# Moving the pooling of a two-block network onto TensorE and reordering its mixer stage

## The chip, the cores and the metric

The kernel runs on one core of a Trainium2 chip. TensorE (PE) does matrix products, VectorE (DVE) and GpSimd (POOL) work on elements, ScalarE (ACT) evaluates functions and copies, SyncE (SP) starts the DMAs that bring weights. The metric is the device time of one execution in microseconds (us). Every engine has its own in-order queue; the queues meet through semaphores only.

## The reference, cut to what matters

Two blocks of two layers each work on one sequence of 512 positions with 1024 channels, in float32. The first block (attention of three kinds) isn't touched except by the padding. In the second block each layer is a feed-forward part, the mixer and a second feed-forward part, each followed by a layer norm. The mixer is what the change concerns:

```python
h = x @ w_in[l]                       # 1024 -> 512 (u) + 4 x 512 (q, f, v, g)
u = h[..., :D_POOL]
q, f_raw, v, g = jnp.split(h[..., D_POOL:], 4, axis=-1)
y_pool = multiscale_pool(u, pool_w[l], pool_scale[l])
o = hgrn2_recurrence(q, f_raw, v, lb_all[l])
y_hgrn = head_rms_norm(o, hgrn_norm_g[l]) * jax.nn.silu(g)
mix = jnp.concatenate([y_pool, y_hgrn], axis=-1) @ w_out[l]
# multiscale_pool, group i of 128 channels, window w = 2, 4, 8, 16:
#   (mean of the last min(w, t+1) positions of u) - u, then a 128x128 product, then a scale per channel
# hgrn2_recurrence, per head: S_t = diag(f_t) S_(t-1) + (1 - f_t) outer v_t;  o_t = S_t^T q_t
```

## The kernel before, in words

Activations lie channels on partitions, positions along the free axis. Each large product is made of tiles of 128 output channels by 512 positions. Weights and activations are split into a high and a low float32r part, and a tile takes three matmuls per 128 input channels (three_products, lines 214, 215 and 217), so 24 for the mixer's input (DC = 8). SP fetches weight tiles into a ring of four, DVE splits them two tiles ahead (split_tile, lines 167 and 169), PE multiplies, and in the mixer ACT copies tile i out of bank 6 or 7 into p2 (line 1583). A tile may start when its weights are split and the tile two before it has been copied.

The mixer has 20 input tiles (N_IN2), in the order f (0 to 3), q (4 to 7), v (8 to 11), u (12 to 15, the pooled half), g (16 to 19). Between the tiles every engine does parts of the recurrence, at tile numbers written out by hand ("if i == 13"). The recurrence is computed in four chunks of 128 positions per head. Inside a chunk, decays are handled at seven levels of block sizes LEVELS = (64, 32, 16, 8, 4, 2, 1): DVE subtracts (sub, line 1690), ACT takes exponentials (level_exps, lines 1578 and 1579), DVE multiplies (level, lines 1708 and 1709), and PE forms scores: two top levels of large pieces (top_level, line 1840) and six masked levels (masked_level, line 1860, 64 small matmuls each, five of the levels and the diagonal of k and q), which DVE adds up under masks (accumulate, lines 1716 to 1720) and then copies into place (line 1806). The keys are turned by PE (line 1899) and multiplied with the values (line 1906), DVE chains the states of the chunks (lines 1791 and 1797). Then PE makes the outputs o of four heads (lines 1918 and 1920), ACT squares them (line 1665), PE sums the squares (line 1924), ACT takes logarithm and exponential for the root (lines 1668 and 1672), DVE multiplies (line 1823), ACT and DVE split into high and low (lines 1676 and 1810), and PE multiplies the first two tiles of w_out (lines 214 to 217 again): chunks k = 0 to 3 are the pooled half, 4 to 7 the four heads.

In this kernel the masked levels start only after the last input tile. The pooling is POOL's: from line 1948 it makes the decayed keys, then per group shifted additions, scale and edge correction and the subtraction (lines 1959 to 1968), each waiting for the one before; PE multiplies each group (pool_product, line 1867), and ACT scales it into p2 (line 1637). PE's order after the last tile is: four pool products, masked levels 0 and 1, keys turned, levels 2 and 3, key-value products, levels 4 and 5, outputs and sums, the first two tiles of w_out.

The helper sb in hybrid_kernel pads each named buffer to a multiple of LINE floats, here 32 (128 bytes). In the compiled kernel before, x, xh and xl (and ones) start at 128 bytes past a multiple of 256, and the weight parts two_hi and two_lo, the feed-forward activations hh and hl and the mixer's buffers start at a multiple of 256: the small buffer eps with its padding takes 128 bytes.

Of the kernel before, what the change touches and what calls it, by code (L numbers as in the profile page):

```python
# [21 lines left out]
ALU = mybir.AluOpType  # L22
# [52 lines left out]
M_INV = M_MASK + 32 * len(MASKED)  # L75
N_K2 = M_INV + HH * PADT

# [4 lines left out]
LINE = 32  # L82
# [1425 lines left out]

def mixers(kit, ctx, l, before):

# [4 lines left out]
    def sb(name, shape):  # L1515
# [5 lines left out]
    vrow = sb("vrow", [P, NT, HH, P])  # L1521


    v_place = p2[:, D_V:D_V + HH, :].rearrange("p h t -> p (h t)")
    at = v_place.rearrange("p (n h t) -> p n h t", n=NT, h=HH)
    pl = v_place[:, 0:2 * (PADT + T)].rearrange("p (s t) -> p s t", s=2)

    kd = p2[:, D_F:D_F + HH, :].rearrange("p h t -> p (h t)")

    kr = kd.rearrange("p (n h c) -> p n h c", n=NT, h=HH)  # L1530
    qe = bb[:]

    ad, tm = (kit.ln[:, i, :].rearrange("p (a t) -> p a t", t=32) for i in range(2))
    sta = sb("sta", [P, 3, HH, P])
    el = sb("el", [P, NT * HH])
    lbv = sb("lbv", [P, 6, HH])
# [3 lines left out]
    k_banks = (bank[6], bank[7], bank[3])  # L1540
    s = kit.sems("mix", DENSE + APPLY_SEMS + ("chain_v", "abs_f", "exp_f", "ln_f", "ls_made", "km_made", "k_made", "a_made", "m_made", "lb_in",
                         "lb_act", "lb_made", "e2", "e3", "e4", "b_made", "sub_made", "exp_made", "top_mm", "last_sub", "ke_exp", "sc_kept", "lv_made",
                         "lev_mm", "acc_made", "at_made", "v_turned", "v_kept", "qe_exp", "qe_made", "kd_made",
                         "k_turned", "k_kept", "kv_mm", "st_made", "o_mm", "o_kept", "osq_made", "o_summed",
                         "oln_made", "orstd_made", "y_made", "g_made", "u_pad", "pool_chain", "pooled", "p_mm",
                         "hi_made", "p_kept", "lo_made", "ylo_made", "zeroed"))
# [6 lines left out]
    rst = df[:, 0, :]  # L1553

# [10 lines left out]
    def scalar(a):  # L1565
# [6 lines left out]
        a.activation(lbv[:, 1, :], lbv[:, 1, :], ACT.Exp, scale=-1.0).then_inc(s["lb_act"], 1)  # L1572

        def level_exps(i):
# [4 lines left out]
            a.activation(left, left, ACT.Exp, scale=-1.0).then_inc(s["exp_made"], 1)  # L1579

        for i in range(N_IN2):
# [8 lines left out]
            if i == 4:  # L1590
                a.wait_ge(s["lb_act"], 2)
                a.activation(lbv[:, 1, :], lbv[:, 1, :], ACT.Ln, bias=kit.ones[:, 0:1]).then_inc(s["lb_act"], 1)
                a.wait_ge(s["exp_f"], 1)
                a.activation(df[:, 0, :], df[:, 0, :], ACT.Ln, bias=kit.ones[:, 0:1]).then_inc(s["ln_f"], 1)
            if i == 5:
# [6 lines left out]
            if i == 6:  # L1602
                a.wait_ge(s["e2"], HH)
                a.activation(df[:, 1, :], df[:, 1, :], ACT.Exp, scale=-1.0).then_inc(s["e3"], 1)
            if i == 7:
# [5 lines left out]
            if i == 8:  # L1611
                a.wait_ge(s["e3"], 1)
                a.activation(df[:, 1, :], df[:, 1, :], ACT.Ln, bias=kit.ones[:, 0:1]).then_inc(s["e4"], 1)
            if i == 12:
                level_exps(0)

                for n in range(NT):
                    a.wait_ge(s["v_turned"], n + 1)
                    a.activation(vrow[:, n, :, :], bank[n][:].rearrange("p (h c) -> p h c", h=HH), ACT.Copy
                                 ).then_inc(s["v_kept"], 1)  # L1620
            if i == 13:
                level_exps(1)
            if i == 14:

                a.wait_ge(s["last_sub"], 1)
                a.activation(v_place, v_place, ACT.Exp).then_inc(s["ke_exp"], 1)
                a.activation(el[:], bb[:, P - 1:W:P], ACT.Exp).then_inc(s["ke_exp"], 1)
            if i == 15:
# [623 lines left out]
```

## Time and profile before

| | before |
|---|---|
| median of 3 runs | 2828.55 us (2828.39 to 2829.93) |
| the profiled execution | 2831.76 us |
| its span, first to last instruction | 2830.0 us |
| mean granted TensorE clock | 0.958 of full speed |
| PE busy | 2630.8 us (93%) |
| DVE, ACT, POOL busy | 48%, 26%, 24% |

Times in the rows are us from the first instruction. A row of a timeline holds consecutive instructions of one line: the start, the time from the first start to the last end, the engine, the line, the operation, what it writes and reads, the shapes and their number; in brackets the idle time of the engine before it and what ended that. A float32 matmul (not float32r) counts as two instructions. In a row of a stretch each engine has its busy time and its instructions in brackets, and PEclk is the granted TensorE clock as a share of 2.4 GHz.

### The profile page before, as it was taken

How to read it: one execution, taken by the hardware profiler on the slowest of the kernel's cores; microseconds unless marked ns; L12 is line 12 of the kernel's file. 1: busy time of each engine (PE TensorE's matmuls, PEld its weight loads, DVE VectorE, ACT ScalarE, POOL GpSimd, SP SyncE). 2: the span in 40 equal slices, each digit the busy share in tenths (PEclk: the TensorE clock that was granted, in tenths of full speed). 3: DMA queues.
4: the chain of work that ended last, by engine and by line, in shares of the span. 5: the costliest groups of instructions: out<-in, count | busy, mean ns of one | idle time of the engine just before them, and what ended most of it. 6: DMA issues, size and time to landing. Idle time of an engine off the chain costs nothing. (4 is left out here: it accounts for less than half of the span.)

```text
span 2830.0 us, 36447 instructions
## 1 busy us (share of the span) xinstructions
PE 2630.8 (93%) x13232; PEld 2086.7 (74%) x13232; DVE 1367.0 (48%) x2271; ACT 727.9 (26%) x1465; POOL 685.3 (24%) x422
## 2 busy tenths in 40 slices
PE   7989888989879999997799999899999987999997
PEld 4867756867648888876678888788888765788886
DVE  4356834367653334467653333533344575633344
ACT  2135621156431110042431110211110424311101
POOL 1000031000223331117243331233311163433311
PEclk9998989979989999999899999999999997999999
DMA  5310013300122333221122333133332220223332
GB/s 193 97 45 1 2 60 126 96 1 2 38 89 92 94 102 102 78 84 58 39 81 90 96 108 102 56 97 96 99 103 88 75 67 31 79 93 96 103 103 80
DMA packets 57268, 222.22 MB, mean 79 GB/s; under 512 B 6664, under 2 KB 7816, under 8 KB 56768
## 3 DMA queue, kind: packets, MB, share of 16 engines
q1 hardware_dynamic: 56000, 214.01, 23.7%
q10 hardware_dynamic: 1152, 6.68, 0.6%
q8 instruction: 72, 1.18, 0.2%
q14 instruction: 44, 0.36, 0.0%
HBM read 218.51 MB, written 2.15 MB: 78 GB/s over the span
## 5 line engine op out<-in xcount | busy, mean ns | idle before, releaser
L214 PE MATMUL bank<-xh,two_hi 128*128 128x512 f32 x1856 | 741.5, 400 | 37.7 <-ACT xh L1173 33.7
L215 PE MATMUL bank<-xh,two_lo 128*128 128x512 f32 x1856 | 737.8, 398 | 0.0
L217 PE MATMUL bank<-xl,two_hi 128*128 128x512 f32 x1856 | 727.0, 395 | 0.0
L167 DVE CAST two_hi<-two_raw 128x1024 fp32r<-128x1024 f32 (+1 forms) x292 | 228.3, 782 | 952.7 <-PE bank L217 950.7
L214 PEld LDWEIGHTS bank<-xh,two_hi 128*128 128x128 f32 x1856 | 352.5, 190 | 129.3 <-issue 36.6
L215 PEld LDWEIGHTS bank<-xh,two_lo 128*128 128x128 f32 x1856 | 352.8, 190 | 82.0 <-issue 0.5
L217 PEld LDWEIGHTS bank<-xl,two_hi 128*128 128x128 f32 x1856 | 351.0, 189 | 82.7
L169 DVE TENSOR_TENSOR two_lo<-two_raw,two_hi 128x1024 fp32r<-128x1024 f32 (+1 forms) x292 | 395.5, 1355 | 10.0
L1395 POOL TENSOR_TENSOR up_hm<-up_sg,up_hm 128x512 f32<-128x512 f32 x88 | 197.9, 2249 | 581.2 <-ACT up_hm L1377 581.2
L214 PE MATMUL bank<-hh,two_hi 128*128 128x512 f32 x704 | 276.3, 392 | 0.0
L217 PE MATMUL bank<-hl,two_hi 128*128 128x512 f32 x704 | 274.1, 389 | 0.0
L215 PE MATMUL bank<-hh,two_lo 128*128 128x512 f32 x704 | 274.0, 389 | 0.0
L214 PE MATMUL bank<-xh,onein_hi 128*128 128x512 f32 x384 | 154.3, 402 | 16.6 <-ACT xh L470 15.8
L1377 ACT ACTIVATE up_hm<-bank 128x512 f32<-128x512 f32 x88 | 52.8, 600 | 428.1 <-PE bank L217 428.1
L215 PE MATMUL bank<-xh,onein_lo 128*128 128x512 f32 x384 | 153.7, 400 | 0.0
L215 PEld LDWEIGHTS bank<-hh,two_lo 128*128 128x128 f32 x704 | 132.1, 188 | 28.4 <-issue 1.0
L214 PEld LDWEIGHTS bank<-hh,two_hi 128*128 128x128 f32 x704 | 132.2, 188 | 28.1 <-issue 1.0
L217 PEld LDWEIGHTS bank<-hl,two_hi 128*128 128x128 f32 x704 | 132.1, 188 | 27.7
L217 PE MATMUL bank<-xl,onein_hi 128*128 128x512 f32 x384 | 150.7, 398 | 1.5 <-POOL xl L500 1.5
L1398 POOL TENSOR_TENSOR hl<-up_hm,hh 128x512 f32 x88 | 115.0, 1307 | 83.7 <-ACT hh L1379 83.7
L937 ACT ACTIVATE w<-w,negm 128x128 f32<-128x128 f32 (+4 forms) x192 | 94.9, 494 | 97.2 <-DVE negm L880 96.1
L1379 ACT ACTIVATE hh<-up_hm 128x512 f32 x88 | 55.7, 633 | 216.1 <-POOL up_hm L1395 216.1
(314 smaller groups left out, 3185.6 us busy)
## 6 DMA issues: line engine op xcount, KB each, us to landing
two_raw<-in_up SPq DMA_DIRECT2D x180, 512.0 KB, 3.6
two_raw<-in_down SPq DMA_DIRECT2D x64, 704.0 KB, 4.0
one_raw<-in_w_in SPq DMA_DIRECT2D x52, 512.0 KB, 3.6
two_raw<-in_w_in SPq DMA_DIRECT2D x40, 512.0 KB, 3.6
one_raw<-in_w_out SPq DMA_DIRECT2D x16, 512.0 KB, 3.6
two_raw<-in_w_out SPq DMA_DIRECT2D x16, 512.0 KB, 3.7
w<-in_w ACTq DMA_DIRECT2D x2, 2048.0 KB, 10.6
x<-in_x SPq DMA_DIRECT2D x1, 2048.0 KB, 8.3
```

The lines of the kernel that those rows point to most:

```text
L167: v.tensor_copy(st.hi[:, h, 0:w], st.raw[:, r, 0:w]).then_inc(st.hi_made, 1)
L169: v.tensor_tensor(st.lo[:, h, 0:w], st.raw[:, r, 0:w], st.hi[:, h, 0:w].bitcast(F32), ALU.subtract).then_inc(st.w_split, 1)
L214: pe.matmul(out[:], wh, xh[:, kx, :], start=start, stop=False)
L215: pe.matmul(out[:], wl, xh[:, kx, :], start=False, stop=False)
L217: return pe.matmul(out[:], wh, xl[:, kx, :], start=False, stop=stop)
L937: a.activation(row, row, ACT.Exp, bias=negm[:, i:i + 1], scale=-1.0, accum_out=tot[:, i:i + 1]).then_inc(s["exps"], 1)
L1377: a.activation(hm[:, f, :], bank[1][:], ACT.Copy).then_inc(s["out_taken"], 1)
L1379: a.activation(hh[:, bass.ds(j * 2 + f, 1), :].rearrange("p o t -> p (o t)"), hm[:, f, :], ACT.Copy).then_inc(s["hhi_made"], 1)
L1395: g.tensor_tensor(hm[:, f, :], sg[:, f, :], hm[:, f, :], ALU.mult).then_inc(s["h_made"], 1)
L1398: g.tensor_tensor(hl[:, at, :].rearrange("p o t -> p (o t)"), hm[:, f, :], hh[:, at, :].rearrange("p o t -> p (o t)").bitcast(F32), ALU.su ...
```

## The change

The pooling becomes products on TensorE. A constant kb (128 x 4 x 272 floats, fetched by ACT's DMA queue at tile 8) holds for each window the banded matrix "mean minus token": one for the first chunk, one for the others, and 16 columns for what spills from the chunk before. pool_weights multiplies u by the group's weights first (16 matmuls of 128x128), ACT copies the four banks into p2, and pool_steps then applies the band: per group four matmuls of 128 columns and three of 16. The scaled result is taken straight from PSUM by ACT (high part) and DVE (low part). POOL loses the pooling, the decayed keys (now 16 exponentials on ACT with a bias and one product on DVE), the product of q with its decay (now DVE) and the low parts; it keeps two memsets.

The masked levels move between the input tiles, one after each of tiles 14 to 18, in the order of levels 2, 3, the diagonal, 4, 5, 6; one remains after tile 19. Values are turned after tiles 12 and 13, keys after tile 16, pool_weights after tile 17. DVE's and ACT's steps move up accordingly. The last accumulate writes into place directly. After the state chain PE makes chunks k = 0 to 3 of the first two w_out tiles, then the heads' outputs and sums (two banks instead of four for the sums, so a sum waits for the logarithm two before it), then k = 4 to 7. ACT takes logarithm, exponential and high part head by head instead of in three rounds. PE's loop over tiles 8 to 11 is written out. LINE becomes 64 (256 bytes).

Of the diff, the lines that matter (removed lines are left out where the step only moved):

```diff
-LINE = 32
+LINE = 64
...
+    MASKED_LEVELS = (2, 3, None, 4, 5, 6)
+    MASK_OF = (0, 1, 5, 2, 3, 4)
...
             if i == 8:
+                a.dma_start(kb[:], kit.d["kb"]).then_inc(s["steps"], 16)
+                a.wait_ge(s["b_made"], HH * NT)
+                for b in range(HH * NT):
+                    c = slice(b * P, (b + 1) * P)
+                    a.activation(kd[:, c], bb[:, c], ACT.Exp, scale=-1.0, bias=bb[:, b * P + P - 1:b * P + P]
+                                 ).then_inc(s["ke_exp"], 1)
+                a.activation(el[:], bb[:, P - 1:W:P], ACT.Exp).then_inc(s["ke_exp"], 1)
+                level_exps(0)
+            if i == 9:
+                level_exps(1)
+            if i == 11:
+                level_exps(2)
             if i == 12:
+                level_exps(3)
+                keep_values(0)
+                keep_values(1)
+            if i == 13:
+                keep_values(2)
+                keep_values(3)
+                level_exps(4)
+            if i == 14:
+                level_exps(5)
+            if i == 15:
+                a.wait_ge(s["zeroed"], 2)
+                a.wait_ge(s["top_mm"], 2 * NT)
                 for n in range(NT):
+                    top = bank[n][:].rearrange("p (h t) -> p h t", h=HH)
+                    a.activation(at[0:64, n, :, 64:128], top[0:64, :, 64:128], ACT.Copy).then_inc(s["at_made"], 1)
+                    a.activation(at[0:32, n, :, 32:64], top[0:32, :, 32:64], ACT.Copy).then_inc(s["at_made"], 1)
+                    a.activation(at[64:96, n, :, 96:128], top[64:96, :, 96:128], ACT.Copy).then_inc(s["at_made"], 1)
+            if i == 16:
+                a.wait_ge(s["k_turned"], NT - 1)
+                for n in range(NT - 1):
+                    a.activation(kr[:, n, :, :], bank[n][:].rearrange("p (h c) -> p h c", h=HH), ACT.Copy
+                                 ).then_inc(s["k_kept"], 1)
             if i == 17:
+                level_exps(6)
+                a.activation(qe, bb[:], ACT.Exp).then_inc(s["qe_exp"], 1)
+                a.wait_ge(s["z_mm"], NT)
+                for n in range(NT):
+                    a.activation(zt[:, n, :], bank[n][:], ACT.Copy).then_inc(s["z_kept"], 1)
...
+        for c in range(HH):
+            a.wait_ge(s["p_mm"], c + 1)
+            a.activation(kit.xh[:, c, :], bank[6 + c % 2][:], ACT.Copy, scale=kit.s2[:, Q_PS + c:Q_PS + c + 1]
+                         ).then_inc(s["hi_made"], 1)
...
+            if i == 8:
                 v.wait_ge(s["b_made"], HH * NT)
                 v.wait_ge(s["k_made"], HH)
                 sub(0)
+            if i == 9:
                 sub(1)
                 v.wait_ge(s["out_taken"], 2 + D_Q + HH)
                 level(0)
+            if i == 10:
+                level(1)
+            if i == 11:
+                sub(2)
+                sub(3)
+            if i == 12:
+                level(2)
+                v.wait_ge(s["ke_exp"], HH * NT)
+                v.tensor_tensor(kd, kk[:], kd, ALU.mult).then_inc(s["kd_made"], 1)
+            if i == 13:
+                level(3)
+                sub(4)
             if i == 14:
+                sub(5)
             if i == 15:
+                level(4)
+                accumulate(0)
             if i == 16:
+                level(5)
+                accumulate(1)
             if i == 17:
+                sub(6)
+                accumulate(2)
             if i == 18:
+                level(6)
+                accumulate(3)
             if i == 19:
+                v.wait_ge(s["qe_exp"], 1)
+                v.tensor_tensor(qe, qe, q, ALU.mult).then_inc(s["qe_made"], 1)
+                accumulate(4)
+        accumulate(5)
...
+        for c in range(HH):
+            v.wait_ge(s["hi_made"], c + 1)
+            v.scalar_tensor_tensor(kit.xl[:, c, :], bank[6 + c % 2][:], kit.s2[:, Q_PS + c:Q_PS + c + 1],
+                                   kit.xh[:, c, :].bitcast(F32), ALU.mult, ALU.subtract).then_inc(s["lo_made"], 1)
...
+        def turn_keys():
+            pe.wait_ge(s["kd_made"], 1)
+            pe.wait_ge(s["at_made"], 3 * NT)
+            for n in range(NT - 1):
+                for h in range(HH):
+                    mm = pe.transpose(bank[n][:, h * P:(h + 1) * P], kd[:, cols(h, n)], ident)
+                mm.then_inc(s["k_turned"], 1)
+        def pool_weights():
+            pe.wait_ge(s["k_kept"], NT - 1)
+            pe.wait_ge(s["out_taken"], 2 + D_U + HH)
+            for n in range(NT):
+                for c in range(HH):
+                    mm = pe.matmul(bank[n][:, c * P:(c + 1) * P], p2[:, D_U + c, n * P:(n + 1) * P],
+                                   kit.s2[:, Q_PW + c * P:Q_PW + (c + 1) * P], start=True, stop=True)
+                mm.then_inc(s["z_mm"], 1)
+        def pool_steps(c):
+            out = bank[6 + c % 2]
+            for n in range(NT):
+                first = FIRST_STEP if n == 0 else INNER_STEP
+                mm = pe.matmul(out[:, n * P:(n + 1) * P], zt[:, n, c * P:(c + 1) * P], kb[:, c, first:first + P],
+                               start=True, stop=n == 0)
+                if n:
+                    mm = pe.matmul(out[:, n * P:n * P + PADT], zt[:, n - 1, c * P:(c + 1) * P],
+                                   kb[:, c, SPILL_STEP:SPILL_STEP + PADT], start=False, stop=True)
+            mm.then_inc(s["p_mm"], 1)
...
+        dense_products(pe, st, s["out_taken"], l, "w_in_2", DC, kit.xh, kit.xl, dense_banks, first=D_Q, last=D_V)
+        for i in range(D_V, N_IN2):
             dense(i)
+            if i == 11:
+                top_level(0)
+            if i == 12:
+                top_level(1)
+                turn_values(0)
+                turn_values(1)
+            if i == 13:
+                turn_values(2)
+                turn_values(3)
+            if i == 14:
+                masked_level(0)
+            if i == 15:
+                masked_level(1)
+            if i == 16:
+                masked_level(2)
+                turn_keys()
+            if i == 17:
+                masked_level(3)
+                pool_weights()
+            if i == 18:
+                masked_level(4)
+        masked_level(5)
+        pe.wait_ge(s["z_kept"], NT)
         for n in range(NT - 1):
             for h in range(HH):
+                mm = pe.matmul(bank[n][:, h * P:(h + 1) * P], kr[:, n, h, :], vrow[:, n, h, :], start=True, stop=True)
             mm.then_inc(s["kv_mm"], 1)
+        pe.wait_ge(s["steps"], 16)
+        pe.wait_ge(s["out_taken"], 2 + N_IN2)
+        for c in range(HH):
+            if c >= 2:
+                pe.wait_ge(s["lo_made"], c - 1)
+            pool_steps(c)
+        after = base + N_IN2
+        def out_products(k):
+            for u in range(2):
+                mm = three_products(pe, st, bank[u], u, k, kit.xh, kit.xl, k, k == 0, k == DC - 1)
+                if k == DC - 1:
+                    mm.then_inc(st.mm_done, 1)
+        def sum_squares(h):
+            pe.wait_ge(s["osq_made"], h + 1)
+            if h >= 2:
+                pe.wait_ge(s["oln_made"], h - 1)
+            pe.matmul(bank[6 + h % 2][:], kit.ones[:], osq[:, h * T:(h + 1) * T], start=True, stop=True
+                      ).then_inc(s["o_summed"], 1)
+        pe.wait_ge(st.w_split, st.split_after(l, after + 1))
         pe.wait_ge(s["st_made"], 1 + 2 * HH)
+        for k in range(HH):
+            pe.wait_ge(s["lo_made"], k + 1)
+            out_products(k)
         pe.wait_ge(s["qe_made"], 1)
         pe.wait_ge(s["at_made"], 3 * NT + 4)
         for h in range(HH):
             for n in range(NT):
+                out = bank[2 + h][:, n * P:(n + 1) * P]
                 mm = pe.matmul(out, vrow[:, n, h, :], at[:, n, h, :], start=True, stop=n == 0)
                 if n:
                     mm = pe.matmul(out, sta[:, n - 1, h, :], qe[:, cols(h, n)], start=False, stop=True)
             mm.then_inc(s["o_mm"], 1)
             if h:
+                sum_squares(h - 1)
+        sum_squares(HH - 1)
+        for k in range(HH, DC):
+            pe.wait_ge(s["ylo_made"], k - HH + 1)
+            out_products(k)
...
-        for i, w in enumerate(POOL_WINDOWS):
-            u = p2[:, D_U + i, :]
-            g.wait_ge(s["out_taken"], 2 + D_U + i + 1)
-            link(g.tensor_tensor(pl[:, 0, PADT + 1:], u[:, 1:], u[:, :T - 1], ALU.add))
-            for j in range(1, i + 1):
-                a_, b_ = pl[:, (j - 1) % 2, :], pl[:, j % 2, :]
-                link(g.tensor_tensor(b_[:, PADT:], a_[:, PADT:], a_[:, PADT - 2 ** j:PADT + T - 2 ** j], ALU.add))
-            m = pl[:, i % 2, PADT:]
-            link(g.tensor_scalar(m[:, PADT:], m[:, PADT:], 1.0 / w, None, ALU.mult))
...
-            g.tensor_tensor(u, m, u, ALU.subtract).then_inc(s["pooled"], 1)
-            g.wait_ge(s["pooled"], i + 1)
...
+        inside = (a <= b) & (a > b - w)
+        kb[:, i, FIRST_STEP:FIRST_STEP + P] = inside * (f32(1) / np.minimum(b + 1, w).astype(f32)) - (a == b)
+        kb[:, i, INNER_STEP:INNER_STEP + P] = inside * (f32(1) / f32(w)) - (a == b)
+        kb[:, i, SPILL_STEP:] = (a > P + np.arange(PADT)[None, :] - w) * (f32(1) / f32(w))
```

## Rows read from the trace of the kernel before

**Rows 1.** The page: busy time of each engine, share of span, instructions.
```profile
PE 2630.8 (93%) x13232; PEld 2086.7 (74%) x13232; DVE 1367.0 (48%) x2271; ACT 727.9 (26%) x1465; POOL 685.3 (24%) x422
```

**Rows 2.** Stretches, PE alone: both layers' time from tile 19 to w_out.
```profile
1325.20:1399.20 74.00, 46.22 (x924) 0.77 0.01 2
2322.00:2397.00 75.00, 46.78 (x925) 0.75 0.01 2
```

**Rows 3.** Timeline of ACT: input tiles 18 and 19 copied out, layer 0.
```profile
1319.66 0.60 ACT L1583 ACTIVATE p<-bank 128x512 f32<-128x512 f32 x1 [4.42 <-PE bank L217]
1325.23 0.60 ACT L1583 ACTIVATE p<-bank 128x512 f32<-128x512 f32 x1 [4.98 <-PE bank L217]
```

**Rows 4.** A stretch of all engines (PE, PEld, DVE, ACT, POOL, PEclk) after tile 19.
```profile
1330.00:1345.00 15.00, 3.19 (x4) 1.00 (x4) 4.26 (x2) 0.69 (x1) 14.06 (x14) 0.57 0.00 0
```

**Rows 5.** Timeline of POOL: the last step of the pooling.
```profile
1342.57 1.26 POOL L1968 TENSOR_TENSOR p<-p 128x512 f32<-128x512 f32 x1
```

**Rows 6.** Timeline of PE after the pooling: masked levels, then the first output.
```profile
1346.74 3.14 PE L1860 MATMUL bank<-xx 128*32 128x32 f32 x234 [0.78 <-ACT p L1637]
...
1361.29 0.75 PE L1860 MATMUL bank<-xx 128*32 128x32 f32 x35 [2.59 <-issue]
...
1366.93 1.26 PE L1860 MATMUL bank<-xx 128*32 128x32 f32 x126
...
1370.84 0.72 PE L1860 MATMUL bank<-p,kk 128*32 128x32 f32 x60 [2.02 <-issue]
1375.56 1.20 PE L1918 MATMUL bank<-p,vrow 128*128 128x128 f32 x4 [4.00 <-DVE p L1806]
```

**Rows 7.** Timeline of ACT and PE: outputs, root, and the last matmul of w_out.
```profile
1383.52 0.60 ACT L1665 ACTIVATE xx<-bank 128x512 f32<-128x512 f32 x1 [1.82 <-PE bank L1920]
1385.94 0.60 ACT L1665 ACTIVATE xx<-bank 128x512 f32<-128x512 f32 x1 [1.82 <-PE bank L1920]
1386.43 2.42 ACT L1668 ACTIVATE df<-bank,eps 128x512 f32<-128x512 f32 x4
...
1383.32 1.02 PE L1924 MATMUL bank<-xx,ones 128*128 128x512 f32 x2
...
1398.46 0.39 PE L217 MATMUL bank<-xl,two_hi 128*128 128x512 f32 x1
```

**Rows 8.** Timeline of DVE: a split, a sub, masked add, copy into place, states.
```profile
1280.89 0.69 DVE L167 CAST two_hi<-two_raw 128x1024 fp32r<-128x1024 f32 x1
...
1282.76 2.28 DVE L1690 TENSOR_TENSOR df<-bb 128x2048 f32<-128x2048 f32 x1
...
1368.49 2.35 DVE L1797 SCALAR_TENSOR_TENSOR sta<-sta,el,bank 128x128 f32<-128x128 f32 x8
1370.76 0.68 DVE L1718 TENSOR_TENSOR ln<-bank,k 128x512 f32<-128x512 f32 x1
...
1373.65 1.77 DVE L1806 COPY p<-ln 32x512 f32<-32x512 f32 x4
```

**Rows 9.** Timeline of ACT: one function of a 128x2048 buffer between tiles 8 and 9.
```profile
1258.98 2.00 ACT L1613 ACTIVATE df<-df,ones 128x2048 f32<-128x2048 f32 x1
```

**Rows 10.** Stretches of all engines around a layer norm: PE's pause and what follows.
```profile
1200.50:1205.50 5.00, 1.86 (x9) 1.33 (x9) 3.77 (x9) 4.12 (x11) 2.35 (x1) 1.00 0.14 34
1205.50:1209.00 3.50, 3.40 (x9) 2.20 (x10) 3.43 (x6) 3.45 (x7) 2.56 (x3) 0.56 0.27 107
```

**Rows 11.** DMA queues from 1340 to 1380 us: packets and MB that bring instructions.
```profile
q8 instruction: 6, 0.10, 1.0%
```

**Rows 12.** Timeline of PE, a feed-forward down product; the second is 24 matmuls later.
```profile
1120.29 0.39 PE L214 MATMUL bank<-hh,two_hi 128*128 128x512 f32 x1
...
1125.73 0.39 PE L214 MATMUL bank<-hh,two_hi 128*128 128x512 f32 x1
```

**Rows 13.** The page's costliest groups: dense matmuls by what they read, count, mean ns.
```profile
L214 PE MATMUL bank<-xh,two_hi 128*128 128x512 f32 x1856 | 741.5, 400 | 37.7 <-ACT xh L1173 33.7
...
L214 PE MATMUL bank<-hh,two_hi 128*128 128x512 f32 x704 | 276.3, 392 | 0.0
```

More of the change, by code:

```diff
@@ L1539, in mixers @@
     dense_banks = bank[6:8]
[L1540 to L1546, printed above, removed]
+    s = kit.sems("mix", DENSE + APPLY_SEMS + (
+        "chain_v", "abs_f", "exp_f", "ln_f", "ls_made", "km_made", "k_made", "a_made", "m_made", "lb_in", "lb_act", "lb_made",
+        "e2", "e3", "e4", "b_made", "sub_made", "exp_made", "top_mm", "ke_exp", "lv_made", "lev_mm", "acc_made", "at_made",
+        "v_turned", "v_kept", "qe_exp", "qe_made", "kd_made", "k_turned", "k_kept", "kv_mm", "st_made", "o_mm", "o_kept",
+        "osq_made", "o_summed", "oln_made", "orstd_made", "y_made", "g_made", "z_mm", "z_kept", "p_mm", "hi_made",
+        "lo_made", "ylo_made", "zeroed", "steps"))
     q = p2[:, D_Q:D_Q + HH, :].rearrange("p h t -> p (h t)")
@@ L1752, in vector @@
                 v.tensor_tensor(df[:, 0, :], df[:, 0, :], df[:, 1, :], ALU.add).then_inc(s["a_made"], 1)
-            if i == 10:
+            if i in (6, 7):
                 v.wait_ge(s["a_made"], 1)
-                for h in range(HH):
+                for h in ((0, 1) if i == 6 else (2, 3)):
                     for n in range(NT):
@@ L1870, in tensor @@
         dense_on_arrival(pe, st, s, l, "w_in_2", DC, kit.xh, kit.xl, dense_banks,
                          lambda k: wait_high(pe, s, k), lambda k: wait_low(pe, s, k))
-        dense_products(pe, st, s["out_taken"], l, "w_in_2", DC, kit.xh, kit.xl, dense_banks, first=D_Q, last=D_U)
-        dense(D_U)
-        pe.wait_ge(s["out_taken"], 2 + D_V + HH)
-        for n in range(NT):
-            for h in range(HH):
-                mm = pe.transpose(bank[n][:, h * P:(h + 1) * P], p2[:, D_V + h, n * P:(n + 1) * P], ident)
-            mm.then_inc(s["v_turned"], 1)
@@ L1897, in tensor @@
+        masked_level(5)
+        pe.wait_ge(s["z_kept"], NT)
         for n in range(NT - 1):
             for h in range(HH):
-                mm = pe.transpose(k_banks[n][:, h * P:(h + 1) * P], kd[:, cols(h, n)], ident)
-            mm.then_inc(s["k_turned"], 1)
-        masked_level(2)
-        masked_level(3)
-        for n in range(NT - 1):
-            pe.wait_ge(s["k_kept"], n + 1)
-            for h in range(HH):
-                mm = pe.matmul(bank[n][:, h * P:(h + 1) * P], kr[:, n, h, :], vrow[:, n, h, :],
-                               start=True, stop=True)
-            mm.then_inc(s["kv_mm"], 1)
@@ L1916, in tensor @@
             for n in range(NT):
-                out = bank[h][:, n * P:(n + 1) * P]
+                out = bank[2 + h][:, n * P:(n + 1) * P]
                 mm = pe.matmul(out, vrow[:, n, h, :], at[:, n, h, :], start=True, stop=n == 0)
@@ L1922, in tensor @@
             if h:
-                pe.wait_ge(s["osq_made"], h)
-                pe.matmul(bank[4 + h - 1][:], kit.ones[:], osq[:, (h - 1) * T:h * T], start=True, stop=True
-                          ).then_inc(s["o_summed"], 1)
-        pe.wait_ge(s["osq_made"], HH)
-        pe.matmul(bank[4 + HH - 1][:], kit.ones[:], osq[:, (HH - 1) * T:HH * T], start=True, stop=True
-                  ).then_inc(s["o_summed"], 1)
-        after = base + N_IN2
-        pe.wait_ge(st.w_split, st.split_after(l, after + 1))
```

234 lines of the change are left out of this document (72 added, 162 removed).

## The prediction, made before the changed kernel ran

> **What bounds the kernel now.** I read the page first: PE is busy for 2630.8 of 2830.0 us, 93% [rows 1], so only time in which PE waits, or work taken off it, can be won. The change puts work onto PE. It can pay only where PE stands still now, and the second view, stretches of PE, shows where: from the end of input tile 19 to the first two tiles of w_out the mixer takes 74 us per layer, of which PE is busy 46, at a mean clock of 0.77, and both layers look the same [rows 2]. Third, ACT's timeline dates the tiles: a tile is copied as soon as PE ends it, 18 at 1319.66 and 19 at 1325.23, so one tile is 5.57 us, 24 matmuls of 0.232 us, with no wait between them [rows 3]. Before the tail PE is full; the tail is where it waits.
>
> Fourth, what the tail waits for. From 1330 to 1345 POOL is busy 14.06 of 15 us and PE 3.19, at clock 0.57 [rows 4]: the pooling is the bound. Its last step ends at 1343.8 [rows 5], and only then do the masked levels start, at 1346.7 [rows 6]. From there it is a chain over PE, DVE and ACT with PE mostly at the lower clock: the first output product starts at 1375.56, after 4.00 us of waiting for DVE's last copy [rows 6], and w_out's last matmul ends near 1398.7 [rows 7]. So the tail is 1325.2 to 1398.7, 73.5 us: 50.3 up to the first output, 23.1 from there.
>
> **The change part by part, per layer.** I take the tail apart and build the new one from its rows.
>
> 1. The pooling leaves the path. This removes POOL's wait, PE's four full-width pool products, and the idle time in which the clock fell.
>
> 2. Five masked levels move between tiles 14 to 18. They go where PE is full, so they cost their whole time. A level is 128 instructions. At the full clock 126 of them take 1.26 us, and 234 at a mostly lower one 3.14, or 1.7 per 128 [rows 6]. With some 0.3 for the change of shape I take 1.6 us each: 8.0 us (bounds 6.5 and 10.5). Turning the keys is 12 and pool_weights 32 instructions of 128 columns. The price of one comes from the outputs: heads follow each other every 2.42 us [rows 7], which is 14 such instructions and a sum of squares of about 0.87, so 0.11 us each: 1.3 and 3.5 us. Together 12.9 us.
>
> 3. Instruction supply. The masked levels stop twice for "issue", 2.59 and 2.02 us [rows 6], and 0.10 MB of instructions arrives in six packets in 40 us [rows 11]; a level is 256 instructions with its weight loads. Between dense tiles there is time to fetch, yet one level and a tile are 152 pairs in 7.2 us. Bounds: nothing, or 2.6 us for each of three stops, 7.8. I take 2.0, nearer to nothing, since the dense parts give the fetch about 5.6 us each. So tile 19 ends 14.9 us later than now, near 1340.1.
>
> 4. Do DVE and ACT keep up in the loop? A split takes 1.87 us from start to start [rows 8], a sub or any product over 2048 columns 2.28 [rows 8], an ACT function of that size 2.0 [rows 9]. I let each queue run from tile 3: the tightest place is the split of tile 8, due at 1252.9 and done near 1252.5 after a chain of ACT (exponential, logarithm, absolute value, exponential, logarithm) and DVE's sum; later the worst step on DVE is a split with two subs, 6.4 us, against a tile period that by then has grown to 7 us or more. So I cost this at nothing, with a bound of 3 us if each handoff is slower. ACT's fetch of kb is one DMA issue beside a queue that DMA does not bound, and has 80 us to land: nothing. The two memsets left on POOL are done long before ACT asks for them.
>
> 5. From tile 19 to the outputs. PE needs a masked level (1.6), 24 key-value instructions (2.7) and two pool_steps (8 instructions of 128 columns and 6 of 16, I take 1.2 each). DVE is later: split 1.9, the product of q 2.3, accumulate(4) 1.4, accumulate(5) 0.7 + 1.8, states 0.7 + 2.4, first low part 0.7, in all 11.9 us [rows 8]. pool_steps(2) waits for that low part (lo_made), so PE idles some 5 us here; then pool_steps(2) and (3) 2.4, and 24 matmuls of w_out's pooled half 5.6. At a layer norm PE is busy 1.86 of 5 us, and in the 3.5 us after that the clock is 0.56, near the lower of its two levels (1.2 and 2.4 GHz) [rows 10], so I add 2.0 for a slow start. Sum: 11.9 + 2.4 + 5.6 + 2.0 = 21.9 us; the outputs start near 1362.
>
> 6. From the outputs to the end. Four heads with sums: the last square starts 8.0 us in (now 10.4, because the first two heads run at the lower clock). Then ACT works head by head: logarithm, exponential, high part, 0.6 us each [rows 7] with small handoffs, 1.85 per head; the low part of the last head is ready at about 16.7. The sum of head 2 waits for the logarithm of head 0 behind all four squares, about 1.3 us, which this chain hides. The last chunk of w_out is 1.4 us more, handoffs 0.2. PE idles in pieces, so 1.0 for some time at the lower clock: 19.3 us (bounds 18.3 and 21.5). Now it is 23.1. The pooled half of w_out no longer covers the root, but it would not have been needed: PE now runs its 48 products without a gap, and after the change only the last is behind the root's chain.
>
> Sum per layer: 14.9 + 21.9 + 19.3 = 56.1 against 73.5, a gain of 17.4 us; two layers 34.8. The profiled execution took 2831.76 us, 1.8 more than its span and 3.2 more than the median; the gain does not depend on that, so from the median: 2828.5 - 34.8 = **2793.7**.
>
> 7. The padding. It moves every buffer behind eps by 128 bytes against multiples of 256: the weight parts and hh and hl, not xh and xl. The trace shows two speeds of the same dense matmul. Reading hh, 24 take 5.44 us, 0.2267 each [rows 12]; reading xh, 0.232 [rows 3], and the page's mean durations agree, 392 against 400 ns [rows 13]. Before, hh starts at a multiple of 256 and xh 128 bytes past one. If the moving operand's start decides, hh becomes slow too: 3 x 704 = 2112 matmuls by 5.5 ns, 12 us lost. If it is that both operands share the same remainder, xh becomes fast: at least 3 x 1856 = 5568 by 5.5 ns, 31 us gained, and more with the first block. If it is something else (the loops differ, and so does where the buffers lie), nothing. I take nothing, because no row separates these, and keep both ends.
>
> A rule that speaks against step 2: the Trainium skill, "TensorE: Matmul & The Clock Gate", section "Wait — 56ns, not 53.3ns?", states that matmuls never start closer than about 25 ns however small they are. By it a level would be at least 3.2 us, the five moved ones 16 instead of 8, and the forecast 16 us higher for both layers, an estimate of 2810. The trace's 126 instructions in 1.26 us, 10 ns apart, speak against the rule here [rows 6].
>
> **The rivals.** A, the other speed: the padding slows hh's products. For it: the only buffers at a multiple of 256 that are read as moving operand by dense matmuls are the fast ones. Against: the code around them differs as well. It gives 2793.7 + 12 = 2806. B, the padding speeds up xh's: 2793.7 - 31 = 2763 or a little less. C, the small matmuls don't fit between the tiles: fetch stops of 7.8 us instead of 2.0, levels at 2.1 us (2.5 more), 3 us of DVE and ACT being late: 11.3 per layer more, 2816. For it: the stops in rows 6; against: dense tiles of 5.6 us beside each level. D, slower than before: the coupled queues. ACT now holds waits for DVE (sub_made, b_made) in front of the copy that frees PE's bank, and DVE holds waits for ACT and PE in front of the split PE needs. If a handoff is late in each turn, PE loses it at every tile: the gain of 17.4 per layer is eaten once each of the 15 tiles from 5 to 19 is late by more than 1.2 us; at 1.6 us the kernel is at 2828.5 + 2 x (15 x 1.6 - 17.4) = 2842. Against: before, with the same ring, the tiles show no such wait [rows 3], and by hand each queue arrives before it is due. E, it doesn't do what it says, the pooling stays the bound: excluded, as POOL's pooling is gone.
>
> **How the numbers follow.** Forecast with a neutral padding 0.54, A 0.18, B 0.12, C 0.10, D 0.06. The forecast's own bounds, steps 2, 3, 5 and 6, are about 5 us per layer to either side, 2783 to 2804. The range takes in A and C and the lower side of the forecast and leaves out B and D: 2776 to 2816. A difference of 0.2% is 5.7 us, about what a measurement of this kernel can tell from none. Faster by over 0.2% means under 2822.9: all of the forecast, A, B and most of C, 0.91; within 0.2% 0.04; slower 0.05.
>
> **What would show it.** Tile 19 should be copied about 15 us later after tile 11 than now, with tile periods near 7.2 us at tiles 15 to 18; a period over 9 us means C or D, and the wait before line 217 or 214 then names DVE or ACT. PE should idle some 5 us before pool_steps(2), waiting for DVE, and the time from tile 19's copy to w_out's last matmul should be near 41 us. Of the padding, the start-to-start time of dense matmuls reading hh (0.2267) and xh (0.232) decides A and B at once. The prediction would be wrong above all if those change, or if PE is stopped for instructions beside the dense tiles.

## The result and the profile after

The changed kernel takes 2759.84 us, the median of five runs (2757.37 to 2764.68). The kernel before, in five runs beside it, takes 2829.2 (2828.39 to 2831.14). The ratio is 0.976, with a 95% interval of 0.9746 to 0.9773: 69.4 us gained, twice the forecast 34.8, and 16 us below the lower end of the range. The profiled execution took 2759.84, its span is 2758.1 us and the mean granted clock 0.964.

The page of the kernel after. The engine line answers to [rows 1], the groups to [rows 13].

```profile
PE 2595.6 (94%) x13392; PEld 2090.5 (76%) x13392; DVE 1355.0 (49%) x2281; ACT 735.0 (27%) x1495; POOL 560.4 (20%) x354
...
L213 PE MATMUL bank<-xh,two_hi 128*128 128x512 f32 x1856 | 734.8, 396 | 40.6 <-ACT xh L1172 33.9
L214 PE MATMUL bank<-xh,two_lo 128*128 128x512 f32 x1856 | 729.2, 393 | 0.0
...
L213 PE MATMUL bank<-hh,two_hi 128*128 128x512 f32 x704 | 276.2, 392 | 0.0
```

PE has 160 instructions more and is yet busy 35 us less. Moving work onto PE can't do that, and the mean clock is hardly higher (0.964 for 0.958). The same work has become cheaper: the mean of the xh group fell from 400 to 396 ns, the hh group stayed at 392. The mean duration hides the size, since a matmul overlaps the next. The start-to-start time shows it, here from the timeline of PE of the kernel after, two rows 24 matmuls apart:

```profile
1489.26 0.39 PE L216 MATMUL bank<-xl,two_hi 128*128 128x512 f32 x1
...
1494.70 0.39 PE L216 MATMUL bank<-xl,two_hi 128*128 128x512 f32 x1
```

That is 5.44 us, 0.2267 each, where a tile on xh took 5.57 before [rows 3]. The speed that hh alone had [rows 12] is now everybody's. A weight load takes 190 ns in the mean in both kernels; only the spacing has changed.

The stretches of all engines from tile 19's copy to the mixer's end, for both layers (columns PE, PEld, DVE, ACT, POOL, then PEclk), answer to [rows 2]:

```profile
1317.70:1364.00 46.30, 37.60 (x321) 31.06 (x320) 22.87 (x35) 17.23 (x24) 0.00 (x0) 0.85 0.00 1
2283.70:2329.90 46.20, 37.68 (x320) 31.09 (x318) 22.86 (x35) 17.23 (x24) 0.00 (x0) 0.85 0.00 1
```

The tail is 46.3 and 46.2 us instead of some 74, the clock 0.85 instead of 0.77 and 0.75, and POOL does nothing in it. I cut layer 0's mixer into four pieces, from tile 3's copy to the first addition of the next phase: tiles 3 to 11, 44.8 us before and 44.0 after; tiles 11 to 19, 49.9 and 61.0; tile 19 to the outputs, 50.3 and 26.8; the outputs to the next phase, 23.6 and 19.6. Together 168.7 and 151.4, a gain of 17.4. This includes the faster matmuls: 384 for tiles 4 to 19 and 48 for w_out, by 5.5 ns, would be 2.4 us, which leaves 15.0 for the reordering. Measured at equal padding, from tile 3's copy to ACT's first table load of the next phase, it gains a little more. With the new padding (the padding alone against the changed kernel, both run below) the two layers take 166.5 and 167.2 us, and 151.3 both: 15.2 and 15.9. With the old one (the kernel before against the reordering alone) they take 168.7 and 168.6, and 152.2 and 152.9: 16.4 and 15.7. So the reordering is worth 31 to 32 us in all. The other 37 to 38 us of the 69.4 fall to the padding, and the count agrees within 2 us: 7104 matmuls on xh and xl (3 x 1856, 3 x 384 and 384 of w_out in the first block) by 5.5 ns are 39.1.

### The profile page after: what moved, and what is told of

It is laid out like the page before. It is cut to its first block and busy times, and to the rows that moved or that the text cites. A ratio compares the mean times of both kernels' runs of the same rounds, so it can differ in the third digit from the quotient of the medians.

```text
span 2758.1 us, 36735 instructions
## 1 busy us (share of the span) xinstructions
PE 2595.6 (94%) x13392; PEld 2090.5 (76%) x13392; DVE 1355.0 (49%) x2281; ACT 735.0 (27%) x1495; POOL 560.4 (20%) x354
## 5 line engine op out<-in xcount | busy, mean ns | idle before, releaser
L214 PE MATMUL bank<-xh,two_lo 128*128 128x512 f32 x1856 | 729.2, 393 | 0.0
L216 PE MATMUL bank<-xl,two_hi 128*128 128x512 f32 x1856 | 718.4, 391 | 0.0
L166 DVE CAST two_hi<-two_raw 128x1024 fp32r<-128x1024 f32 (+1 forms) x292 | 218.9, 750 | 916.8 <-PE bank L216 915.1
L213 PE MATMUL bank<-xh,onein_hi 128*128 128x512 f32 x384 | 152.3, 397 | 17.3 <-ACT xh L469 16.4
L214 PEld LDWEIGHTS bank<-hh,two_lo 128*128 128x128 f32 x704 | 132.2, 188 | 28.3 <-issue 1.0
L214 PE MATMUL bank<-xh,onein_lo 128*128 128x512 f32 x384 | 151.4, 394 | 0.0
```

Source lines behind the costliest of these rows:

```text
L166: v.tensor_copy(st.hi[:, h, 0:w], st.raw[:, r, 0:w]).then_inc(st.hi_made, 1)
L213: pe.matmul(out[:], wh, xh[:, kx, :], start=start, stop=False)
L214: pe.matmul(out[:], wl, xh[:, kx, :], start=False, stop=False)
L216: return pe.matmul(out[:], wh, xl[:, kx, :], start=False, stop=stop)
```

## The experiments

**The theories.** Theory 1: a dense matmul is fast when its moving operand and its weights start at the same remainder of 256 bytes. Theory 2: it is the moving operand's start alone that counts (rival A of the prediction). Theory 3: the speed belongs to the loops, and the padding does nothing. Before, xh and xl start 128 bytes past a multiple of 256, and the weights and hh at one. In the changed kernel all of them start 128 past.

**The padding alone**, in the kernel before:

```diff
-LINE = 32
+LINE = 64
```

> The kernel before with the 256-byte padding alone: xh and the weight parts now both start 128 bytes past a multiple of 256. Theory (equal remainders of both operands make the dense matmul fast): all 7104 dense matmuls that read xh or xl go from about 0.232 to 0.2267 us, hh's stay at 0.2267, and the kernel gains 7104 x 0.0057 = 40 us, to about 2790. Rival A (a moving operand that starts at a multiple of 256 is fast): hh goes to 0.232, xh stays, 12 us slower, 2841. Rival neutral: the gain lies in the mixer alone, 2829.

Measured: 2792.5 us against 2826.54 of the kernel before on the same chip, ratio 0.9882 (0.9853 to 0.991). PE of this kernel, two rows 24 matmuls apart, 5.44 us:

```profile
1489.23 0.39 PE L217 MATMUL bank<-xl,two_hi 128*128 128x512 f32 x1
...
1494.67 0.39 PE L217 MATMUL bank<-xl,two_hi 128*128 128x512 f32 x1
```

One constant gives half of the gain: 34.0 us, with an interval of 25 to 42 that holds the 39.1 of the count. Theory 3 falls.

**The reordering alone**, in the changed kernel:

```diff
-LINE = 64
+LINE = 32
```

> The changed kernel with the old 128-byte padding. Theory (the padding is worth about 40 us and the mixer what was forecast): dense matmuls on xh back at 0.232, total near 2829 - 33 = 2796, mixer stage 15 to 17 us shorter per layer than before. Rival (all of the gain is the mixer): 2760. The sum of this gain and that of the padding alone should be the whole 69 us if the two don't depend on each other.

Measured: 2797.5 us, ratio 0.99 (0.9869 to 0.993), that is 28.3 us gained (20 to 37). 24 matmuls on xh are back at 5.58 us:

```profile
1489.13 0.40 PE L214 MATMUL bank<-xh,two_lo 128*128 128x512 f32 x1
...
1494.71 0.39 PE L214 MATMUL bank<-xh,two_lo 128*128 128x512 f32 x1
```

The two halves multiply to 0.978, beside 0.976 measured for both together: they hardly touch each other. The forecast's 34.8 for the reordering is inside the interval, but the 31 to 32 of the traces are nearer to its middle.

**Everything at a multiple of 256** (the kernel before, with 256-byte padding):

```diff
+        ctx.enter_context(nc.sbuf_tensor("lead", [P, 32], F32))
         kit.x = sb(ctx, "x", [P, DC, T])
```

> The kernel before with 256-byte padding and 128 bytes ahead of x, so that x, xh, xl, the weight parts and hh all start at a multiple of 256. Theory of equal remainders: as with the padding alone, 2790, every dense matmul at 0.2267. Rival (it is the remainder 128 of the weight parts, or of all, that makes it fast): xh's matmuls slow at 0.232 or hh's changed, and 2829 or more.

Measured: 2791.05 us, ratio 0.9885 (0.9855 to 0.9915), the same as with everything 128 past. The absolute remainder is worth nothing.

**xh at a multiple of 256, weights and hh 128 past** (the kernel before with the lead buffer alone):

```diff
 LINE = 32
...
+        ctx.enter_context(nc.sbuf_tensor("lead", [P, 32], F32))
         kit.x = sb(ctx, "x", [P, DC, T])
```

> The kernel before with 128 bytes ahead of x alone, which moves everything by 128: x, xh, xl start at a multiple of 256, the weight parts and hh 128 bytes past one. The distance between xh and the weights is as before, both absolute starts are exchanged. Theory of equal remainders: as before, 2829, xh at 0.232, hh at 0.2267. Rival A (moving operand at a multiple of 256 is fast): xh at 0.2267, hh at 0.232, gain 40 - 12 = 28 us, 2801.

Measured: 2827.7 us, ratio 0.9995 (0.9975 to 1.0014). xh, now at the remainder that theory 2 calls the good one, stays slow, 5.58 us for 24, and hh, now at the bad one, stays fast, since it moved together with its weights. Theory 2 falls.

```profile
1489.28 0.40 PE L217 MATMUL bank<-xl,two_hi 128*128 128x512 f32 x1
...
1494.86 0.39 PE L217 MATMUL bank<-xl,two_hi 128*128 128x512 f32 x1
```

**hh moved away from its weights**, in the kernel with 256-byte padding:

```diff
+        ctx.enter_context(sb(f"hpad{i}", [P, 32], F32))
         self.hh = ctx.enter_context(sb(f"hh{i}", [P, FC, T], F32R))
```

> The padding alone, with 128 bytes more ahead of hh: hh and hl start at a multiple of 256, the weight parts 128 bytes past one, xh as with the padding alone. Theory (it is the distance between the moving operand and the weights, modulo 256, whichever buffer moves): the 2112 dense matmuls that read hh go from 0.2267 to about 0.232, those on xh stay at 0.2267, and the kernel is 2112 x 0.0057 = 12 us slower than with the padding alone, near 2804. Rival (what was slow belongs to xh or to the weights alone): hh stays fast, 2792.

Measured: 2798.08 us, ratio 0.99 (0.9886 to 0.9915). The trace is sharper than the medians. This is PE in a down product, where 24 matmuls took 5.44 us before [rows 12] and now take 5.58:

```profile
1110.07 0.39 PE L217 MATMUL bank<-hl,two_hi 128*128 128x512 f32 x1
...
1115.65 0.40 PE L217 MATMUL bank<-hl,two_hi 128*128 128x512 f32 x1
```

For 2112 matmuls that is 12 us. The medians stand 5.6 us above those of the padding alone, and the two intervals overlap, so the cost in total time is less well known than its sign in the trace.

**Distances other than 128**, in the kernel with 256-byte padding: weights 64 bytes from xh, and 32 from hh.

```diff
+        ctx.enter_context(sb(f"hpad{i}", [P, 8], F32))
...
-        kit.eps = sb(ctx, "eps", [P, 2])
+        kit.eps = ctx.enter_context(nc.sbuf_tensor("eps", [P, 2], F32))
+        ctx.enter_context(nc.sbuf_tensor("eps_pad", [P, 8], F32))
```

> The padding alone, but the buffers behind eps start 64 bytes past xh's remainder modulo 256 (192 against 128), and hh 32 bytes past the weights'. Theory 1 (any distance that is no multiple of 256 costs): both kinds of matmul at 0.232 or slower, the kernel near 2792 + 52 = 2844. Theory 2 (only a distance of 128 modulo 256 costs): both at 0.2267, 2792. Theory 3 (smaller distances cost more, the old padding to 128 was a cure for that): both above 0.235, 2860 or more.

Measured: 2850.01 us, ratio 1.0077 (1.0062 to 1.0092), slower than the kernel before. PE on xl, and in a down product on hh, each two rows 24 matmuls apart, 5.60 us both:

```profile
1489.29 0.39 PE L217 MATMUL bank<-xl,two_hi 128*128 128x512 f32 x1
...
1494.89 0.39 PE L217 MATMUL bank<-xl,two_hi 128*128 128x512 f32 x1
...
1110.26 0.40 PE L214 MATMUL bank<-hh,two_hi 128*128 128x512 f32 x1
...
1115.86 0.40 PE L214 MATMUL bank<-hh,two_hi 128*128 128x512 f32 x1
```

All 9216 dense matmuls at 6.7 ns more than 0.2267 would be 61 us over the kernel with the padding alone; measured are 57.5. So 32 and 64 bytes cost at least as much as 128. Of the distances run (0, 32, 64 and 128 bytes, modulo 256) only 0 is fast.

**The first pause in the tail.** PE stood 5.94 us before pool_steps(2). Theory: groups 2 and 3 reuse banks 6 and 7, so they wait for lo_made, and the low part stands on DVE behind the product of q, two accumulates and the states. Rival: the pause costs nothing, since the outputs wait for DVE's accumulates anyhow. Two edits take it away in different ways. First, four banks instead of two:

```diff
+    pool_bank = (bank[6], bank[7], bank[3], bank[4])
...
-            out = bank[6 + c % 2]
+            out = pool_bank[c]
...
-            if c >= 2:
-                pe.wait_ge(s["lo_made"], c - 1)
+            if c == 3:
+                pe.wait_ge(s["acc_made"], 8)
```

> The changed kernel, but the four pooled groups go to four PSUM banks (6, 7, 3, 4) instead of 6 and 7 in turn, so pool_steps(2) and (3) no longer wait for a low part. Theory (PE's pause of 5.9 us before pool_steps(2) and the lower clock after it cost about 10 us per layer): the two steps run at full clock before the pause, but PE then still waits for DVE's states and first low part, so the outputs start about 6 us earlier per layer, 2760 - 12 = 2748. Rival (DVE's chain is the bound, the pause only moves): 0 to 4 us in all.

Measured: 2747.69 us, ratio 0.9717 (0.9699 to 0.9736). The four pool_steps run through, and the wait is now behind them; PE's first matmul of w_out, and PE by stretches (busy, then PEclk):

```profile
1332.06 0.47 PE L213 MATMUL bank<-xh,two_hi 128*128 128x512 f32 x1 [2.31 <-DVE xl L1842]
...
1330.00:1335.00 5.00, 2.94 (x9) 0.79 0.02 3
1335.00:1340.00 5.00, 5.00 (x25) 0.87 0.00 0
```

The pause fell from 5.94 to 2.31 us, and the clock in the 5 us that hold it and in the next 5 is 0.79 and 0.87 instead of 0.50 for 10 us. The rival falls.

**DVE's order**, with the banks as they were: the states and the low parts before accumulate(5) and the product of q, which the outputs alone need.

```diff
             if i == 19:
-                v.wait_ge(s["qe_exp"], 1)
-                v.tensor_tensor(qe, qe, q, ALU.mult).then_inc(s["qe_made"], 1)
                 accumulate(4)
-        accumulate(5)
...
+        accumulate(5)
+        v.wait_ge(s["qe_exp"], 1)
+        v.tensor_tensor(qe, qe, q, ALU.mult).then_inc(s["qe_made"], 1)
```

> The changed kernel with another order on DVE after tile 19: accumulate(4), states, low parts of the pooled half, and only then accumulate(5) and the product of q. Theory (DVE's place for the low part is what PE waits for): the pause before pool_steps(2) all but goes, the clock stays up, the outputs start near 1335 instead of 1344.5, bound by the product of q; 10 us per layer, 2740. Rival (the outputs are bound by DVE's sum of work in any order): under 3 us per layer, 2755.

Measured: 2750.06 us, ratio 0.9723 (0.9702 to 0.9743). Here PE's clock stays at 1.00 and the pause before pool_steps(2) is gone, but the median is no better than with four banks, and half of what was expected beyond the changed kernel is missing. From ACT's table load after tile 19 to that of the next phase are 37.7 us instead of 45.7, so the trace has 16 us for both layers where the ratios have some 10. The table below shows that the tail is not where the rest went. The product of q is now the last before the outputs, as the bracket says:

```profile
1339.71 0.71 PE L2005 MATMUL bank<-p,vrow 128*128 128x128 f32 x4 [1.76 <-DVE bb L1842]
```

**Both edits together.**

> Both edits, four banks and the other order on DVE. Theory: hardly more than the order alone, 2738, since the first low part comes before pool_steps(2) would wait. If the banks alone had shown most of the gain, this should be about as fast as that.

Measured: 2743.04 us (2740.95 to 2743.41), ratio 0.97 (0.9684 to 0.9716), the best kernel of this study. Its stretch from tile 19 to the mixer's end:

```profile
1313.80:1350.90 37.10, 32.49 (x320) 26.34 (x313) 22.85 (x35) 17.18 (x24) 0.00 (x0) 1.00 0.00 1
```

It is 37.1 us instead of 46.3, and with the same work PE's busy time fell from 37.60 to 32.49. Of the 9.2 us, 5.1 are that the same instructions ran at the full clock, and the other 4.1 are idle time gone.

The medians of these kernels mix the tail with differences of some us that arise elsewhere. The traces keep them apart. The tail, from tile 19's copy to ACT's first table load of the next phase, in us:

| kernel | layer 0 | layer 1 | tile 19 copied, layer 0 | median |
|---|---|---|---|---|
| changed | 46.3 | 46.3 | 1317.75 | 2759.84 |
| four banks | 39.8 | 39.8 | 1318.92 | 2747.69 |
| DVE's order | 38.3 | 38.3 | 1321.08 | 2750.06 |
| both edits | 37.2 | 37.2 | 1313.75 | 2743.04 |
| pooled half behind (next) | 45.3 | 45.4 | 1310.18 | 2760.46 |

No edit acts before tile 19 of layer 0, and yet its copy lies at times up to 11 us apart in these executions. In the tail, DVE's order is 1.5 us per layer better than four banks, and both together gain only 1.1 more per layer, as was expected ("hardly more than the order alone"). The 7 us between the medians of the last two edits are mostly not the tail's.

**The pooled half behind the heads.** The change's description says "ahead"; is the order itself worth anything? In the changed kernel the 24 matmuls of chunks 0 to 3 go behind the last sum of squares.

```diff
-        for k in range(HH):
-            pe.wait_ge(s["lo_made"], k + 1)
-            out_products(k)
-
+        pe.wait_ge(s["lo_made"], HH)
...
         sum_squares(HH - 1)
+        for k in range(HH):
+            pe.wait_ge(s["lo_made"], k + 1)
+            out_products(k)
```

> The changed kernel with the products of w_out's pooled half behind the outputs and sums, as before the change. Theory by the rows: the outputs start 6 us earlier but at the lower clock, and the 24 products then fill part of the root's chain and end 4 to 5 us after it: 2760 within 4 us, so putting them ahead is worth nothing by itself. Rival 1 (ahead is worth its place, since it warms the clock and leaves only the last chunk behind the root): 4 to 6 us slower per layer, 2770. Rival 2 (they are better hidden behind the outputs): 3 to 5 us faster per layer, 2752.

Measured: 2760.46 us, ratio 0.9768 (0.9751 to 0.9785): no difference from the changed kernel. In the traces the tail is 0.9 us per layer shorter, which is too little for the medians to show. Behind, the pooled half covers the root's chain; ahead, it covers DVE's last steps. That the two holes are about equal is read from the times, no run took one of them away. PE starts its outputs with a row that the changed kernel doesn't have there; the second row is DVE's last low part:

```profile
1331.09 1.19 PE L2002 MATMUL bank<-p,vrow 128*128 128x128 f32 x4 [1.72 <-issue]
...
1330.13 0.75 DVE L1841 SCALAR_TENSOR_TENSOR xl<-bank,s,xh 128x512 fp32r<-128x512 f32 x1 [2.24 <-ACT xh L1682]
```

The bracket says "issue", but the edit makes PE wait for that low part (lo_made, HH) before the outputs. The low part ends at 1330.88, and PE starts 0.21 us later. So this pause is a wait for DVE and not one of the stops that step 3 priced.

## Why the prediction was wrong

**The step that failed is 7, the padding.** It laid out three cases, gave the price of each, took "nothing, because no row separates these", and chose a range that left B out. B is what happened. Its price was also short: it counted the 5568 matmuls of the second block at 31 us and put the first block's 1536 down as "and more"; they add 8.4. With 31 to 32 for the reordering and 39.1 by count for the padding, the median before of 2828.5 gives 2757 to 2758, where 2759.84 was measured.

Could the rows have decided it? Two facts were at hand: the same dense matmul, engine, line and shape has two speeds [rows 12 and 3], and the difference that could be read off the operands was the remainder, unequal for the slow ones and equal for the fast. A neutral padding left 5.5 ns on each of several thousand matmuls without a mechanism. A chance of 0.12 for B against 0.54 for "neutral" treated the lack of a separating row as evidence for zero. It was evidence for none of the three.

**The reordering, step by step.** The mechanism was right: the pooling left the path, and each later piece sits where it was put. Sizes, per layer, read in layer 0:

Step 1, right. POOL is at 20% and is idle in the tail.

Step 2, nearly right: 12.2 measured, 12.9 forecast. In the timeline of PE of the kernel after, in the loop:

```profile
1285.18 1.30 PE L1907 MATMUL bank<-xx 128*32 128x32 f32 x128
1292.08 1.30 PE L1907 MATMUL bank<-p,kk 128*32 128x32 f32 x128
1293.31 1.53 PE L1915 MATMUL bank<-k,p 128*128 128x128 f32 x12
...
1300.25 1.30 PE L1907 MATMUL bank<-xx 128*32 128x32 f32 x128
1301.48 3.84 PE L1923 MATMUL bank<-s,p 128*128 128x128 f32 x32
...
1310.73 1.30 PE L1907 MATMUL bank<-xx 128*32 128x32 f32 x128
```

From one level's start to the next (1285.18 to 1292.08) are 6.90 us, of which the tile's 24 matmuls are 5.44. A level thus costs 1.46 us between dense tiles, not 1.6: its 128 instructions, and wider spacing of the matmuls around it. Five levels are 7.3 instead of 8.0. With the keys the distance is 8.17, with pool_weights 10.48, so these add 1.3 and 3.6, as forecast.

The Trainium skill, "TensorE: Matmul & The Clock Gate", section "Wait — 56ns, not 53.3ns?", has matmuls start no closer than about 25 ns. These rows disagree: 128 in 1.30 us are 10 ns each, or 20 ns if the two instructions of a float32 matmul are taken as one. These matmuls write 32 output partitions each in turn; whether that is why they start closer was not tested.

Step 3, too dear: no stop for "issue" in the loop, against 2.0 forecast. PE never stands still between tiles 11 and 19 (nor in layer 1, where it is busy for all of 61.00 us too):

```profile
1256.70:1317.70 61.00, 61.00 (x995) 1.00 0.22 66
```

The same eight tiles took 49.9 us before; with the 1.1 us that the padding saves in them, the insertions cost 12.2, not 14.9, and the pieces above add up to just that. One such stop does occur, in layer 1, in the level after tile 19: 1.01 us. The pause that follows it is shorter by about as much (4.74 us), so it cost nothing.

Step 4, right. At tile 8, which the prediction named as the tightest, PE waited 0.18 us for the split, and for nothing else there:

```profile
1234.66 0.50 PE L213 MATMUL bank<-xh,two_hi 128*128 128x512 f32 x1 [0.18 <-DVE two_lo L168]
```

Step 5, too cheap by 4.9 us: 21.9 forecast, 26.8 measured. PE, from the timeline of the kernel after:

```profile
1318.87 2.94 PE L1969 MATMUL bank<-vrow,p 128*128 128x128 f32 x24
1321.65 0.61 PE L1931 MATMUL bank<-kb,p 128*128 128x128 f32 x4
...
1323.13 0.69 PE L1931 MATMUL bank<-kb,p 128*128 128x128 f32 x4
...
1330.78 1.22 PE L1931 MATMUL bank<-kb,p 128*128 128x128 f32 x4 [5.94 <-DVE xl L1841]
...
1336.78 0.77 PE L213 MATMUL bank<-xh,two_hi 128*128 128x512 f32 x1
...
1341.56 0.39 PE L216 MATMUL bank<-xl,two_hi 128*128 128x512 f32 x1
...
1344.55 0.60 PE L2005 MATMUL bank<-p,vrow 128*128 128x128 f32 x4
```

The pause was foreseen with its place and cause ("some 5 us"). What follows it was not: two pool_steps take 6.0 us instead of 2.4, and the 24 matmuls of w_out 7.8 instead of 5.6. Stretches of PE alone (busy, then PEclk) show why:

```profile
1325.00:1330.00 5.00, 0.00 (x0) 0.78 0.00 0
1330.00:1335.00 5.00, 4.22 (x20) 0.50 0.00 0
1335.00:1340.00 5.00, 5.00 (x18) 0.50 0.02 3
1340.00:1344.50 4.50, 4.50 (x18) 0.84 0.00 0
```

PE works without a gap from 1330.8 on, and is at the lower of its two levels (0.50, 1.2 GHz) until after 1340. Step 5 gave this 2.0 us, from a layer norm after which the clock read 0.56 for 3.5 us [rows 10]; it measured 5.4. At the full clock, before the pause, a pool_steps takes 1.48 us (1321.65 to 1323.13), so two are 3.0, and 24 matmuls are 5.4: 6.0 + 7.8 - 3.0 - 5.4. That row's stretch ends after 3.5 us, so it couldn't say how long the lower clock lasts. The pool_steps themselves were priced 0.6 too low (2.4 for two) and the 24 matmuls 0.2 too high. The remaining 1.1 us is DVE's last masked addition, priced from a plain copy in [rows 8]:

```profile
1324.06 2.82 DVE L1750 TENSOR_TENSOR p<-ln 32x512 f32<-32x512 f32 x4
```

It adds and writes into place, 2.82 instead of the copy's 1.77.

Step 6, right in size, with some luck: 19.3 forecast. From 1344.55 to w_out's last matmul, which starts at 1363.39 and lasts 0.39, are 19.2 us. DVE's last two low parts, PE at the last but one chunk of w_out, and the stretch of all engines:

```profile
1360.01 1.48 DVE L1847 TENSOR_TENSOR xl<-xx,xh 128x512 fp32r<-128x512 f32 x2
...
1360.75 0.50 PE L213 MATMUL bank<-xh,two_hi 128*128 128x512 f32 x1
...
1344.50:1363.80 19.30, 16.74 (x89) 11.86 (x88) 8.28 (x12) 9.41 (x16) 0.00 (x0) 1.00 0.00 0
```

The last low part is ready 16.9 us in, where 16.7 was forecast. The 1.0 us for the lower clock never came, as the clock is 1.00 throughout. In its place two chunks of w_out, not one, stand behind the last two low parts, which end within 0.8 us of each other: from the last low part to the end are 2.3 us instead of 1.6.

The sum: 17.4 forecast, plus 2.7 (steps 2 and 3), minus 4.9 (step 5), with 0.2 to 0.3 less from the rest, is 15.0 by count, and 15.2 to 16.4 as measured at equal padding. Errors of opposite sign left the reordering only 1 to 2 us short per layer; that it came so near is in part luck. C and D didn't occur, as PE didn't stand between the tiles. The prediction's own mark for them, a period over 9 us, was set wrongly: tile 18 is copied 10.5 us after tile 17, and that is 5.44 of tile, 1.46 of level and 3.58 of pool_weights, all work. Why the distance between two operands modulo 256 bytes sets the pace was not found; the runs show that it does.

## What to carry to other kernels

When one instruction form shows two start-to-start times in one trace, list what differs in its operands, addresses included, and give each explanation with a mechanism a real chance; a neutral outcome needs a reason too. Here a single padding constant was worth 34 us, so it pays to time it alone before it is bundled with a reordering. A pause of PE is priced with the work that follows it at the lower clock: here a pause of 5.94 us cost another 5.4, and freeing the waited-for result earlier (another bank, another order on DVE) won most of both back.

## What the runs showed of the hardware

- A 128x128 by 128x512 float32r matmul starts every 0.2267 us (24 in 5.44) when moving operand and weights start at equal remainders of 256 bytes, whether both are at 0 or both at 128. With 128 bytes between them 24 take 5.57 to 5.60 us, with 32 or 64 bytes 5.60.
- After 5.94 us without work the granted clock was 0.50 for about 10 us although PE was busy. In layer 1 a pause of 4.74 us was followed by 0.50 as well (2296.7 to 2306). With a pause of 2.31 us the 5 us that hold it and the next 5 read 0.79 and 0.87; in the kernel with both edits a pause of 1.79 us left it at 1.00.
- A masked level, 128 instructions of 32 columns (64 float32 matmuls), takes 1.30 us in the middle of dense tiles and lengthens the tile period by 1.46 us, from 5.44 to 6.90.
